# Sliding-window attention of a four-layer float32 kernel: keys and values from one feature-major product, values transposed, and a new order of projections and first scores

## The chip, the cores and the metric

The kernel runs on one core of a Trainium2 chip. The metric is the device time of one execution in microseconds (us), lower is better. The time before is 2381.49 us, the median of three runs (2381.35 to 2385.41).

## The reference, cut to what matters

The program computes a stack of transformer layers over 512 tokens of width 1024, all in float32. One of them is a mixer with causal sliding-window attention: 16 query heads of 64, two key/value heads (each shared by 8 query heads), a window of 128 tokens and one sink logit per head. Its input projection `w_in` has 1024 + 128 + 128 columns: queries, keys, values.

```python
def swa_sink_mixer(h, w_in, b_in, sinks, w_out, b_out):
    proj = h @ w_in + b_in
    q, k, v = jnp.split(proj, [1024, 1152], axis=-1)
    ...
    s = jnp.einsum('bnqkgd,bnskd->bnkgqs', q, kb) * (64 ** -0.5)
    s = jnp.where(valid[None, :, None, None], s, -jnp.inf)
    mx = jnp.maximum(jnp.max(s, axis=-1, keepdims=True), sink)
    e = jnp.exp(s - mx)
    p = e / (jnp.sum(e, axis=-1, keepdims=True) + jnp.exp(sink - mx))
    o = jnp.einsum('bnkgqs,bnskd->bnqkgd', p, vb)
    return o.reshape(B, T, 1024) @ w_out + b_out
```

Everything else in the program (a gated linear attention mixer, a state space mixer, a second attention mixer and four feed-forward parts) is left as it is.

## The kernel before, in words

**Precision.** Each float32 factor of a projection is split into a rounded part and its rest: AH and AL for activations, WH and WL for weights. A product is three matmuls, high by high, high by low, low by high (`three`, line 350).

**Weights.** The weights of the whole program are one stream of slabs of 128 rows and up to 512 columns. SyncE loads slab i into slot i mod 6 of WS (`weight_in`, line 286) once the rest of slab i - 6 is computed; ScalarE rounds it into WH (`weight_hi`, line 300) once slab i - 6 is no longer used; GpSimd computes the rest into WL (`weight_lo`, line 309). ScalarE and GpSimd do this six slabs ahead of TensorE: `weight_steps(put, e, w, name, nk, k0)` puts the slabs that lie six behind the slabs k0 to nk of part `name`. Each engine carries out its instructions in the order written, so where these steps stand among the other work of ScalarE and GpSimd matters.

**Products.** `gemm` (line 329) has two kinds. Kind "F" gives features by tokens: the weights are the stationary operand and 512 tokens move, in a PSUM bank per 128 features. Kind "T" gives tokens by features: 128 tokens are stationary, and the weights' columns move. `tail=n` runs the last n slabs bank by bank rather than slab by slab; `late=True` lets the first two banks start before the other two. `gemm` is a generator that yields after each slab, and the caller may put other work there. `held` names, per bank, what must be over before the bank is written again. BA is the banks 0 to 3, BB 4 to 7.

**The sliding attention.** `pe_swa`, `act_swa`, `dve_swa` and `pool_swa` (lines 1655 to 1761) are written by hand, one per engine. The order of TensorE is: queries 0 to 7 (`swa.q0`, kind F, 8 slabs of 512 columns, banks BB); keys (`swa.k`, kind F, 8 slabs of 256 columns, since each head's 64 columns are loaded twice, so that both halves of the partitions get a copy); queries 8 to 15 (`swa.q1`, kind F, banks BA); steps 0 and 1 of the attention; values (`swa.v`, kind T, 8 slabs of 128 columns, 96 matmuls), with attention step 2 behind slab 5; then steps 3 to 16. ScalarE and VectorE evict each query bank in two halves and two engines: `q_out` (ScalarE, line 1688) and `q_rest` (VectorE, line 1724).

**The attention pipeline.** `Attention` makes 14 pairs of banks of scores. For step u, TensorE (`pe_attention`, line 1469) computes scores u and adds the mask, transposes the first half of the probabilities of u - 2, multiplies the probabilities of u - 3 by the values, and transposes the second half of u - 2. VectorE (`dve_attention`, line 1571) reduces the maxima of u, copies a transposed half of u - 2 where u is odd, and divides the first half of u - 1. ScalarE (`act_attention`, line 1532) puts out a finished group, copies transposed halves of u - 2, and takes the exponentials of u. GpSimd divides the second half.

```python
run(gemm(... "swa.q1" ..., late=True))                   # line 1667
w.wait_ge(ve, "swa.q", 3)
pe_attention(e, w, SWA, held, range(2))
for kc in gemm(e, w, "swa.v", "T", ..., one_bank=True):
    if kc == 5:
        pe_attention(e, w, SWA, held, [2])
```

Of the kernel before, what the change touches and what calls it, by code (L numbers as in the profile page):

```python
# [9 lines left out]
F32 = mybir.dt.float32  # L10
# [21 lines left out]
V_MIXPRE, V_MLPPRE, V_BQ, V_BK, V_PSC, V_CW, V_CB, V_SN, V_QN, V_KN = 0, 16, 32, 40, 42, 46, 94, 106, 114, 118  # L32
NV = 120
R_BG, R_GN, R_BV, R_SINK, R_DTB, R_ALOG, R_DSK, R_FB = 0, 512, 768, 896, 912, 928, 944, 960
NR_ = 968
# [72 lines left out]
def program(nc, d, out):  # L108
    with ExitStack() as ctx:
# [219 lines left out]
        def gemm(e, w, name, kind, src, nk, xs, banks, ready, held, mw=P, head=None, tail=0, one_bank=False, late=False):  # L329

# [10 lines left out]
            def one(kc, m, weight, x, cs=slice(0, T), start=False, stop=False):  # L341
                s, n, b = (i0 + kc) % NS, width(i0 + kc), banks[m]
                if kind == "F":
                    return e.matmul(PS[b][0:mw, cs], weight[:, s, m * mw:(m + 1) * mw], x[:, cs], start=start, stop=stop,  # L344
                                    skip_group_check=head is not None)
                c = m * n if one_bank else 0
                return e.matmul(PS[b][:, c:c + n], x[:, m * P:(m + 1) * P], weight[:, s, 0:n], start=start, stop=stop,  # L347
                                skip_group_check=head is not None or one_bank)

            def three(kc, m):  # L350
                xh, xl = xs[kc]
                one(kc, m, WH, xh, start=kc == 0 and (m == 0 or not one_bank))
# [59 lines left out]
            for m in range(NT if tail else 0):  # L412
                for kc in range(k1, nk):
# [7 lines left out]
                    if kc == nk - 1:  # L421
                        q.then_inc(mm.sem, mm.tick("done", name, m))
                    elif m == NT - 1:
                        q.then_inc(mm.sem, mm.tick("used", i0 + kc))
# [1213 lines left out]
        def swa_group(t, kv):  # L1638
# [3 lines left out]
            def score(e, w, o, h, first):  # L1642
                w.wait_ge(ve, "swa.k", 1)
# [6 lines left out]
                        [sPT[:, j, :] for j in range(4)], [(mm, "done", "swa.v", 3)], True, 4, 0, 2, (ve, "swa.v"))  # L1650
# [4 lines left out]
        def pe_swa(e, w, held):  # L1655
# [5 lines left out]
            def ksrc(kc):  # L1661
                r = slice(kc * P, (kc + 1) * P)
                return [(64 * j, 64, sw[r, 1024 + 64 * (j // 2):1088 + 64 * (j // 2)]) for j in range(4)]
# [1124 lines left out]
```

## Time and profile before

| | before |
|---|---|
| median of 3 runs | 2381.49 us |
| the profiled execution's own time | 2381.4 us |
| span of its profile | 2379.6 us |
| TensorE busy | 2347.7 us (99%) |
| GpSimd, ScalarE, VectorE busy | 1079.5, 932.1, 701.2 us |
| mean granted TensorE clock | 0.999 |

The span runs from the first to the last instruction in the profile; the execution's own time is 1.8 us longer. A busy time is the union of an engine's instructions. The ends of matmuls are modelled and overlap the next start, so the distance of two starts tells what one costs, not its duration. "Idle before" gives the time in which an engine stood still ahead of a row and what ended it. The sliding attention with its projections lies between about 596 and 770 us.

### The profile page before, as it was taken

What the parts mean: (1) busy time and instruction counts of PE and PEld (TensorE: products, weight loads), DVE (VectorE), ACT (ScalarE), POOL (GpSimd) and SP (SyncE); (2) the same over time, 40 slices, a digit from 0 to 9 for tenths busy, and PEclk for the clock granted to TensorE, in tenths of its full rate; (3) what the DMA queues carried; (4) which work ended last, traced back from release to release, by engine and by line L of the source; (5) the groups of instructions that cost most, each with busy time, mean ns of one, the idle gap of its engine ahead of it and who ended that gap; (6) DMA issues with size and microseconds to landing.
All of it is one profiled execution on the core that took longest, in us unless ns stands there. A gap on an engine that the chain in (4) does not pass through costs nothing.

```text
span 2379.6 us, 29305 instructions
## 1 busy us (share of the span) xinstructions
PE 2347.7 (99%) x11545; PEld 1942.4 (82%) x11545; DVE 701.2 (29%) x1155; ACT 932.1 (39%) x1868; POOL 1079.5 (45%) x891
## 2 busy tenths in 40 slices
PE   9999999999999999999999999999999999999998
PEld 7888888888868888888887788888888778888887
DVE  3424320223284210314355331100152474100113
ACT  5524432334474432433445333323233572332331
POOL 5533544443434544454444444444444503544443
PEclk9999999999999999999999999999999999999999
DMA  6311323322312333333321333333233302433332
GB/s 187 86 62 54 117 96 98 98 98 62 89 36 87 113 98 98 93 102 94 93 85 41 98 111 98 98 93 102 88 98 89 80 1 81 132 98 98 95 97 74
DMA packets 161264, 215.08 MB, mean 90 GB/s; under 512 B 38063, under 2 KB 85927, under 8 KB 161127
## 3 DMA queue, kind: packets, MB, share of 16 engines
q1 hardware_dynamic: 157888, 204.10, 28.6%
q10 hardware_dynamic: 3239, 9.11, 1.2%
q8 instruction: 91, 1.49, 0.3%
q14 instruction: 46, 0.38, 0.0%
HBM read 210.53 MB, written 2.10 MB: 89 GB/s over the span
## 4 chain that ended last, share of the span: by engine, by line
PE 93%; DVE 3%; ACT 2%; POOL 1%; issue 1%; DMA 0%; SPq 0%; ACTq 0%; POOLq 0%; DVEq 0%
PE PS L344 44%; PE PS L347 40%; PE PS L1523 1%; PE PS L1501 1%; PE PS L464 1%; PE PS L2372 1%; ACT s_S L1564 0%; DVE X L586 0%; PE PS L2359 0%; DVE AL L499 0%; PE PS L2007 0%; PE PS L1064 0%; PE PS L445 0%; PE PS L1089 0%; PE PS L2363 0%
## 5 line engine op out<-in xcount | busy, mean ns | idle before, releaser
L318 POOL TENSOR_TENSOR WL<-WS,WH 128x512 fp32r<-128x512 f32 (+2 forms) x772 | 981.6, 1281 | 1089.6 <-ACT WH L307 1070.0
L307 ACT ACTIVATE WH<-WS 128x512 fp32r<-128x512 f32 (+2 forms) x774 | 476.6, 622 | 1217.4 <-PE PS L344 606.7
L344 PE MATMUL PS<-AH,WH 128*128 128x512 f32 (+1 forms) x1696 | 589.6, 373 | 2.9 <-ACT AH L481 2.3
L344 PE MATMUL PS<-AL,WH 128*128 128x512 f32 (+1 forms) x1696 | 586.5, 371 | 1.3 <-DVE AL L499 1.3
L344 PE MATMUL PS<-AH,WL 128*128 128x512 f32 x1552 | 581.7, 389 | 0.0
L344 PEld LDWEIGHTS PS<-AH,WH 128*128 128x128 f32 x1696 | 300.5, 188 | 59.5 <-ACT WH L307 2.8
L344 PEld LDWEIGHTS PS<-AL,WH 128*128 128x128 f32 x1696 | 300.6, 188 | 56.7 <-DVE AL L499 1.9
L344 PEld LDWEIGHTS PS<-AH,WL 128*128 128x128 f32 x1552 | 291.0, 188 | 60.6
L347 PE MATMUL PS<-WH,h_HL 128*128 128x512 f32 x864 | 336.1, 389 | 0.0
L347 PE MATMUL PS<-WH,h_HH 128*128 128x512 f32 x864 | 336.1, 389 | 0.0
L347 PE MATMUL PS<-WL,h_HH 128*128 128x512 f32 x864 | 336.1, 389 | 0.0
L347 PE MATMUL PS<-WH,AH 128*128 128x512 f32 (+2 forms) x616 | 229.4, 388 | 0.8 <-ACT g_G L1211 0.5
L347 PE MATMUL PS<-WH,AL 128*128 128x512 f32 (+2 forms) x616 | 224.4, 380 | 1.7 <-DVE AL L492 1.6
L347 PE MATMUL PS<-WL,AH 128*128 128x512 f32 (+2 forms) x616 | 222.1, 379 | 0.0
L347 PEld LDWEIGHTS PS<-WH,h_HL 128*128 128x128 f32 x864 | 162.2, 188 | 33.9
L347 PEld LDWEIGHTS PS<-WH,h_HH 128*128 128x128 f32 x864 | 162.2, 188 | 33.5
L347 PEld LDWEIGHTS PS<-WL,h_HH 128*128 128x128 f32 x864 | 162.2, 188 | 33.4
L826 DVE TENSOR_TENSOR h_HT<-h_HT 128x512 f32<-128x512 f32 x64 | 44.7, 699 | 418.9 <-ACT h_HH L803 418.9
L918 DVE TENSOR_TENSOR h_HT<-PS,h_HT 128x512 f32<-128x512 f32 x44 | 30.2, 687 | 395.0 <-ACT h_HT L893 395.0
L347 PEld LDWEIGHTS PS<-WH,AL 128*128 128x128 f32 x616 | 114.6, 188 | 24.5 <-DVE AL L492 2.6
L347 PEld LDWEIGHTS PS<-WH,AH 128*128 128x128 f32 x616 | 114.4, 188 | 23.6 <-issue 2.5
L347 PEld LDWEIGHTS PS<-WL,AH 128*128 128x128 f32 x616 | 114.7, 188 | 21.3 <-issue 0.7
(353 smaller groups left out, 1899.5 us busy)
## 6 DMA issues: line engine op xcount, KB each, us to landing
WS<-in_mlp_w_up_dram SPq DMA_DIRECT2D x128, 256.0 KB, 2.8
WS<-in_mlp_w_down_dram SPq DMA_DIRECT2D x128, 256.0 KB, 2.6
WS<-in_ffn_w_gate_dram SPq DMA_DIRECT2D x176, 128.0 KB, 2.1
WS<-in_ffn_w_up_dram SPq DMA_DIRECT2D x176, 128.0 KB, 2.2
WS<-in_ffn_w_down_dram SPq DMA_DIRECT2D x88, 256.0 KB, 2.6
WS<-in_gla_w_in_dram SPq DMA_DIRECT2D x48, 256.0 KB, 2.6
WS<-in_even_w_in_dram SPq DMA_DIRECT2D x48, 256.0 KB, 2.6
WS<-in_odd_w_in_dram SPq DMA_DIRECT2D x32, 256.0 KB, 2.7
```

The lines of the kernel that those rows point to most:

```text
L307: e.activation(WH[:, s, 0:n], WS[:, s, 0:n], ACT.Copy).then_inc(hi.sem, hi.tick(i))
L318: e.tensor_tensor(WL[:, s, 0:n], WS[:, s, 0:n], WH[:, s, 0:n].bitcast(F32), ALU.subtract).then_inc(lo.sem, lo.tick(i))
L344: return e.matmul(PS[b][0:mw, cs], weight[:, s, m * mw:(m + 1) * mw], x[:, cs], start=start, stop=stop, skip_group_check=head is not None)
L347: return e.matmul(PS[b][:, c:c + n], x[:, m * P:(m + 1) * P], weight[:, s, 0:n], start=start, stop=stop, skip_group_check=head is not None ...
L464: q = e.transpose(PS[b][:, (2 * c + t) * P:(2 * c + t + 1) * P], src(2 * half + t, 2 * j + c), IDENT)
L826: e.tensor_tensor(HT[:, k, :], HT[:, k, :], HT[:, k, :], ALU.mult).then_inc(ve.sem, ve.tick())
L918: e.tensor_tensor(HT[:, k, :], PS[b[2 + m]][:, :], HT[:, k, :], ALU.mult).then_inc(ve.sem, ve.tick("gated", name, n))
L1501: q = e.transpose(PS[b][:, j * P:(j + 1) * P], S[:, j * P:(j + 1) * P], IDENT)
L1523: q = e.matmul(o.rearrange("p (h n) -> p h n", h=per), G.v(2 * (c + i) + par, kb), p4[par][:, i:i + per, kb, :], start=kb == 0, stop=kb == ...
L2372: e.matmul(o, oMQ[:, h, t * P:W], oMK[:, h, 0:W], start=first, stop=False, skip_group_check=True)
```

## The change

- Keys and values come from one product of kind F (`swa.kv`, 8 slabs of 256 columns, banks 2 and 3, the last four slabs bank by bank). The keys' columns are loaded once, and ScalarE (`sKH`) and VectorE (`sKL`) write each head's keys to both halves of the partitions, in four half-width instructions each in the place of two whole ones.
- ScalarE evicts the values as features into `sVF` (a score buffer that is free then), TensorE transposes them in four instructions behind slab 1 of `swa.q1`, and VectorE copies them to `sV`. The bias is added on ScalarE. The product `swa.v` and its 8 slabs are gone.
- Attention steps 0 and 1 stand behind slabs 2 and 3 of `swa.q1`; its last four slabs then run bank by bank, and steps 2 to 16 follow without other work between.
- ScalarE: `q_out` of banks 0 to 2 behind attention step 1, of bank 3 behind step 2. VectorE: `q_rest` of banks 0 to 2 behind step 1, of bank 3 behind step 2. The weight steps placed at the attention's steps 8 and later are four in the place of six, on ScalarE and GpSimd.

```diff
         def pe_swa(e, w, held):
...
-            run(gemm(e, w, "swa.k", "F", ksrc, 8, AHL, BA[2:4], feats("mlp0"), held))
-            for m in range(2):
-                held[BA[2 + m]] = (ve, "swa.k", m)
-            run(gemm(e, w, "swa.q1", "F", cols(sw, 512, 512), 8, AHL, BA, feats("mlp0"), held, late=True))
+            run(gemm(e, w, "swa.kv", "F", cols(sw, 1024, 256), 8, AHL, BA[2:4], feats("mlp0"), held, tail=4))
+            held[BA[2]] = (ve, "swa.k", 1)
+            held[BA[3]] = (sc, "swa.vf")
+
+            def value_tokens():
+                b = BB[3]
+                w.wait_ge(*held[b])
+                w.wait_ge(sc, "swa.vf")
+                for t in range(NT):
+                    q = e.transpose(PS[b][:, t * P:(t + 1) * P], sVF[:, t * P:(t + 1) * P], IDENT)
+                q.then_inc(mm.sem, mm.tick("swa.v"))
+                held[b] = (ve, "swa.v")
+            for kc in gemm(e, w, "swa.q1", "F", cols(sw, 512, 512), 8, AHL, BA, feats("mlp0"), held, tail=4, late=True):
+                if kc == 1:
+                    value_tokens()
+                elif kc in (2, 3):
+                    pe_attention(e, w, SWA, held, [kc - 2])
             for m in range(4):
                 held[BA[m]] = (ve, "swa.q", 4 + m)
-            w.wait_ge(ve, "swa.q", 3)
-            pe_attention(e, w, SWA, held, range(2))
-            for kc in gemm(e, w, "swa.v", "T", cols(sw, 1152, 128), 8, AHL, [BA[3]] * 4, feats("mlp0"), held, one_bank=True):
-                if kc == 5:
-                    pe_attention(e, w, SWA, held, [2])
-            held[BA[3]] = (ve, "swa.v")
-            w.wait_ge(ve, "swa.q", 6)
-            pe_attention(e, w, SWA, held, range(3, SWA.n + 3))
+            pe_attention(e, w, SWA, held, range(2, SWA.n + 3))
...
         def act_swa(e, w):
...
-            run(weight_steps(weight_hi, e, w, "swa.k", 8))
-            for m in range(2):
-                w.wait_ge(mm, "done", "swa.k", m)
-                e.activation(sKH[:, m, :], PS[BA[2 + m]][:, :], ACT.Identity, bias=vcol(V_BK + m)).then_inc(
-                    sc.sem, sc.tick("swa.k", m))
-            run(weight_steps(weight_hi, e, w, "swa.q1", 8))
-            q_out(1, [3, 0])
-            act_attention(e, w, SWA, [0])
-            q_out(1, [1])
-            act_attention(e, w, SWA, [1])
-            late = weight_steps(weight_hi, e, w, "swa.v", 8)
-            next(late)
-            next(late)
-            q_out(1, [2])
+            run(weight_steps(weight_hi, e, w, "swa.kv", 4))
+            w.wait_ge(mm, "done", "swa.kv", 0)
+            for g in range(2):
+                r = slice(64 * g, 64 * g + 64)
+                for z in (g, 1 - g):
+                    e.activation(sKH[64 * z:64 * z + 64, g, :], PS[BA[2]][r, :], ACT.Identity,
+                                 bias=VC[r, V_BK:V_BK + 1]).then_inc(sc.sem, sc.tick("swa.k", g, z))
+            w.wait_ge(mm, "done", "swa.kv", 1)
+            e.activation(sVF, PS[BA[3]][:, :], ACT.Identity, bias=vcol(V_BV)).then_inc(sc.sem, sc.tick("swa.vf"))
+            run(weight_steps(weight_hi, e, w, "swa.kv", 8, 4))
+            for kc in weight_steps(weight_hi, e, w, "swa.q1", 4):
+                if kc > 1:
+                    act_attention(e, w, SWA, [kc - 2])
+            q_out(1, range(3))
+            late = weight_steps(weight_hi, e, w, "swa.q1", 8, 4)
             for u in range(2, SWA.n + 4):
                 act_attention(e, w, SWA, [u])
+                if u == 2:
+                    q_out(1, [3])
                 if u > 7:
                     next(late, None)
...
         def dve_swa(e, w):
...
-            q_rest(1, [3])
-            dve_attention(e, w, SWA, [0])
-            q_rest(1, [0])
-            dve_attention(e, w, SWA, [1])
-            q_rest(1, [1, 2])
-            dve_attention(e, w, SWA, [2])
-            w.wait_ge(mm, "done", "swa.v", 3)
...
+            w.wait_ge(mm, "swa.v")
+            e.tensor_copy(sV[:, :, :], PS[BB[3]][:, :].rearrange("p (t n) -> p t n", t=NT)).then_inc(
+                ve.sem, ve.tick("swa.v"))
+            dve_attention(e, w, SWA, [0, 1])
+            q_rest(1, range(3))
+            dve_attention(e, w, SWA, [2])
+            q_rest(1, [3])
             dve_attention(e, w, SWA, range(3, SWA.n + 4))
```

VectorE around attention steps 2 and 3, before. L1729 is `q_rest`, L1581 to L1593 the maxima of a step, L1607 to L1627 the division of the step before it, L1744 the values:

```order
L1729 SCALAR_TENSOR_TENSOR s_Q<-PS,VC,s_Q 64x512 x4
L1581 TENSOR_REDUCE SM<-PS 128x2 x2
L1589 SCALAR_TENSOR_TENSOR SM<-SM,NSINK 128x4
L1593 TENSOR_TENSOR SM<-ROWS,SM 128x4
L1607 TENSOR_TENSOR SM<-SM 128x4
L1611 RECIPROCAL SM<-SM 128x4
L1627 TENSOR_TENSOR s_S<-s_S,SM 128x512
L1744 TENSOR_TENSOR s_V<-PS,ROWS 128x512
L1581 TENSOR_REDUCE SM<-PS 128x2 x2
```

The same place with the change, where L1736 is `q_rest`, L1579 to L1591 the maxima and L1605 to L1625 the division:

```order
L1736 SCALAR_TENSOR_TENSOR s_Q<-PS,VC,s_Q 64x512 x6
L1579 TENSOR_REDUCE SM<-PS 128x2 x2
L1587 SCALAR_TENSOR_TENSOR SM<-SM,NSINK 128x4
L1591 TENSOR_TENSOR SM<-ROWS,SM 128x4
L1605 TENSOR_TENSOR SM<-SM 128x4
L1609 RECIPROCAL SM<-SM 128x4
L1625 TENSOR_TENSOR s_S<-s_S,SM 128x512
L1736 SCALAR_TENSOR_TENSOR s_Q<-PS,VC,s_Q 64x512 x2
L1579 TENSOR_REDUCE SM<-PS 128x2 x2
```

Between the division of step 2 and the maxima of step 3 two instructions of `q_rest` (bank 3) now stand where the eviction of the values stood.

ScalarE at the same steps, before. L1564 and L1569 are the exponentials of a step, L307 weights, L1694 `q_out`, L1552 copies of transposed probabilities:

```order
L1564 ACTIVATE s_S,SM<-PS,SM 128x256 x4
L1569 ACTIVATE SM<-SM 128x4
L307 ACTIVATE WH<-WS 128x128 x2
L1694 ACTIVATE s_Q<-PS,VC 64x512 x2
L1552 ACTIVATE s_PT<-PS 128x512 x2
L1564 ACTIVATE s_S,SM<-PS,SM 128x256 x4
L1569 ACTIVATE SM<-SM 128x4
L1552 ACTIVATE s_PT<-PS 128x512
```

With the change, where L1562 and L1567 are the exponentials, L1698 `q_out` and L1550 the copies:

```order
L1562 ACTIVATE s_S,SM<-PS,SM 128x256 x4
L1567 ACTIVATE SM<-SM 128x4
L1698 ACTIVATE s_Q<-PS,VC 64x512 x6
L1550 ACTIVATE s_PT<-PS 128x512 x2
L1562 ACTIVATE s_S,SM<-PS,SM 128x256 x4
L1567 ACTIVATE SM<-SM 128x4
L1698 ACTIVATE s_Q<-PS,VC 64x512 x2
L1550 ACTIVATE s_PT<-PS 128x512
```

`q_out` of bank 3 (L1698 x2) now stands behind the exponentials of step 2.

## Rows read from the trace of the kernel before

**Rows 1.** The page: busy time of the engines, and shares of the last chain by engine

```profile
PE 2347.7 (99%) x11545; PEld 1942.4 (82%) x11545; DVE 701.2 (29%) x1155; ACT 932.1 (39%) x1868; POOL 1079.5 (45%) x891
...
PE 93%; DVE 3%; ACT 2%; POOL 1%; issue 1%; DMA 0%; SPq 0%; ACTq 0%; POOLq 0%; DVEq 0%
```

**Rows 2.** Chain in order of time (start us, us, what): 512-column matmuls, then the values

```profile
410.77 87.04 PE PS L344 x384
...
649.36 7.99 PE PS L347 x72
...
658.81 0.93 PE PS L1501 x8
659.74 2.63 PE PS L347 x24
```

**Rows 3.** Timeline of TensorE (start us, us, what), attention steps 0 to 6, first instructions

```profile
645.54 0.22 PE L1645 MATMUL PS<-s_KH,s_Q 128*128 128x128 f32 x1
...
647.71 0.36 PE L1645 MATMUL PS<-s_KH,s_Q 128*128 128x256 f32 x1
...
649.12 0.31 PE L347 MATMUL PS<-WH,AH 128*128 128x128 f32 x1
...
657.19 0.33 PE L1645 MATMUL PS<-s_KH,s_Q 128*128 128x256 f32 x1
...
658.64 1.09 PE L1501 MATMUL PS<-CK,s_S 128*128 128x128 f32 x8
...
662.20 0.33 PE L1645 MATMUL PS<-s_KH,s_Q 128*128 128x256 f32 x1
...
667.73 0.63 PE L1501 MATMUL PS<-CK,s_S 128*128 128x128 f32 x4 [0.48 <-ACT AH L1540]
...
675.28 0.63 PE L1501 MATMUL PS<-CK,s_S 128*128 128x128 f32 x4 [0.47 <-DVE s_S L1627]
```

**Rows 4.** Timeline of VectorE, attention steps 2 and 3

```profile
658.52 1.53 DVE L1729 SCALAR_TENSOR_TENSOR s_Q<-PS,VC,s_Q 64x512 fp32r<-64x512 f32 x2 [1.96 <-ACT s_Q L1694]
660.08 1.29 DVE L1581 TENSOR_REDUCE SM<-PS 128x2 f32<-128x512 f32 x2
...
662.08 0.69 DVE L1627 TENSOR_TENSOR s_S<-s_S,SM 128x512 f32<-128x512 f32 x1
...
663.63 1.29 DVE L1581 TENSOR_REDUCE SM<-PS 128x2 f32<-128x512 f32 x2 [0.26 <-PE PS L1489]
...
665.88 0.69 DVE L1601 COPY s_PT<-PS 128x512 f32<-128x512 f32 x1 [0.57 <-PE PS L1501]
...
666.89 0.69 DVE L1627 TENSOR_TENSOR s_S<-s_S,SM 128x512 f32<-128x512 f32 x1
```

**Rows 5.** Timeline of ScalarE, attention steps 2 and 3

```profile
657.09 1.39 ACT L1694 ACTIVATE s_Q<-PS,VC 64x512 fp32r<-64x512 f32 x2
659.28 1.09 ACT L1552 ACTIVATE s_PT<-PS 128x512 f32<-128x512 f32 x2 [0.80 <-PE PS L1501]
...
665.15 0.48 ACT L1564 ACTIVATE s_S<-PS,SM 128x256 f32<-128x256 f32 x1 [0.27 <-DVE SM L1589]
...
667.06 0.60 ACT L1540 ACTIVATE AH<-PS 128x512 fp32r<-128x512 f32 x1
```

**Rows 6.** Timeline of ScalarE, weight slabs rounded while the keys' product runs

```profile
619.14 2.82 ACT L307 ACTIVATE WH<-WS 128x256 fp32r<-128x256 f32 x6
```

**Rows 7.** Timeline of GpSimd, rests of the same slabs

```profile
619.63 8.94 POOL L318 TENSOR_TENSOR WL<-WS,WH 128x256 fp32r<-128x256 f32 x8 [5.24 <-ACT WH L307]
```

**Rows 8.** Chain in order of time, ScalarE at attention step 12

```profile
701.82 1.82 ACT s_S L1564 x8
703.74 0.52 ACT WH L307
```

**Rows 9.** Timeline of TensorE, the row behind its longest idle

```profile
706.71 0.63 PE L1501 MATMUL PS<-CK,s_S 128*128 128x128 f32 x4 [1.94 <-ACT s_S L1564]
```

**Rows 10.** Windows: us, busy PE, PEld, DVE, ACT, POOL, PEclk, DMA share, GB/s

```profile
700.00:710.00 10.00, 7.39 (x58) 4.93 (x54) 9.08 (x19) 8.33 (x27) 6.16 (x6) 1.00 0.18 56
```

More of the change, by code:

```diff
@@ L325, in weight_steps, with gemm @@
                 yield kc
-        def gemm(e, w, name, kind, src, nk, xs, banks, ready, held, mw=P, head=None, tail=0, one_bank=False, late=False):
+        def gemm(e, w, name, kind, src, nk, xs, banks, ready, held, mw=P, head=None, tail=0, late=False):
             if name not in first:
@@ L345, in one @@
                                     skip_group_check=head is not None)
-                c = m * n if one_bank else 0
-                return e.matmul(PS[b][:, c:c + n], x[:, m * P:(m + 1) * P], weight[:, s, 0:n], start=start, stop=stop,
-                                skip_group_check=head is not None or one_bank)
+                return e.matmul(PS[b][:, 0:n], x[:, m * P:(m + 1) * P], weight[:, s, 0:n], start=start, stop=stop,
+                                skip_group_check=head is not None)
             def three(kc, m):
                 xh, xl = xs[kc]
-                one(kc, m, WH, xh, start=kc == 0 and (m == 0 or not one_bank))
+                one(kc, m, WH, xh, start=kc == 0)
                 if kind == "F":
@@ L411, in gemm @@
                 yield kc
-            for m in range(NT if tail else 0):
+            for m in range(count(k1) if tail else 0):
                 for kc in range(k1, nk):
@@ L422, in gemm @@
                         q.then_inc(mm.sem, mm.tick("done", name, m))
-                    elif m == NT - 1:
+                    elif m == count(kc) - 1:
                         q.then_inc(mm.sem, mm.tick("used", i0 + kc))
@@ L1642, in score @@
             def score(e, w, o, h, first):
-                w.wait_ge(ve, "swa.k", 1)
+                w.wait_ge(ve, "swa.k", kv)
+                w.wait_ge(ve, "swa.q", 4 * kv + 3)
                 q, ks = sQ[:, 8 * kv + h, t * P:(t + 1) * P], slice(k0 * P, k0 * P + W)
@@ L1649, in program @@
         SWA = Attention("swa", [swa_group(t, kv) for kv in range(2) for t in range(NT)], [sS[:, j, :] for j in range(6)],
-                        [sPT[:, j, :] for j in range(4)], [(mm, "done", "swa.v", 3)], True, 4, 0, 2, (ve, "swa.v"))
+                        [sPT[:, j, :] for j in range(4)], [(mm, "done", "swa.q1", 3)], True, 4, 0, 2, (ve, "swa.v"))
+        sVF = sS[:, 5, :]
         def hn(name):
@@ L1751, in pool_swa @@
         def pool_swa(e, w):
-            for part in ("swa.q0", "swa.k", "swa.q1"):
-                run(weight_steps(weight_lo, e, w, part, 8))
-            late = weight_steps(weight_lo, e, w, "swa.v", 8)
-            next(late)
-            next(late)
+            for part, nk in (("swa.q0", 8), ("swa.kv", 8), ("swa.q1", 4)):
+                run(weight_steps(weight_lo, e, w, part, nk))
+            late = weight_steps(weight_lo, e, w, "swa.q1", 8, 4)
             for x in range(SWA.n):
```

28 lines of the change are left out of this document (12 added, 16 removed).

## The prediction, written before the changed kernel was run

> **What bounds the kernel now.** I read the page first. TensorE is busy 2347.7 of 2379.6 us and holds 93% of the chain that ended last, so a change gains where it takes work from TensorE and no wait comes in its place [rows 1]. Next the chain in order of time over the stage: matmuls of 512 columns follow each other 87.04 / 384 = 0.227 us apart, and the product of the values is on the chain too, as pieces of 7.99 and 2.63 us [rows 2]. Last the timelines of the engines around attention steps 2 and 3, since the steps are a pipeline through four engines and the change moves its fill: the starts of each step on TensorE [rows 3], and what VectorE and ScalarE do for it [rows 4, 5]. The reader is to see there that the attention runs at about 3.8 us a step (two steps from 667.73 to 675.28, with only 0.47 us idle at the second [rows 3]): TensorE bounds it, but barely, so work on TensorE that is lost can't be made up later, and a hole stays a hole.
>
> **The change, part by part.** I count us from the start of a step's scores. All of it is set against the profiled execution: 2381.4 us, 1.8 us over its span, which is also the median (2381.49) within 0.1 us.
>
> *The values' product goes.* 96 matmuls take 7.99 + 2.63 = 10.6 us on the chain [rows 2]. They move only 128 columns each and still start 10.62 / 96 = 0.111 us apart. Keys and values now take 8 slabs of two banks, 48 matmuls of 512 columns, exactly what the keys took alone: nothing is added there. The Trainium skill ("TensorE: Matmul & The Clock Gate", section "Wait — 56ns, not 53.3ns?") has warm back-to-back matmuls of 128 columns start 55.6 ns apart. By that figure, as an estimate, the product would be worth 96 x 0.0556 = 5.3 us and the whole gain 5.3 us smaller; the trace's distance is twice that and the measurement is what I use.
>
> *Four transposes come in.* Eight take 0.93 us [rows 2], so four with a changeover take about 0.6 us. They wait for the eviction of the values as features, priced below.
>
> *Steps 0 and 1 move into `swa.q1`.* Their work stays: 2.17 us (645.54 to 647.71) and 1.41 us (to 649.12) [rows 3]. Their exponentials and divisions now lie beside the last four slabs, 48 matmuls of 512 columns: 48 x 0.227 = 10.9 us (12 for each bank, 2.72 us). That covers the softmax of both. Step 2 begins when these end: 645.54 + 0.6 + 2.17 + 1.41 = 649.7, against 657.19 before, 7.5 us earlier.
>
> *Step 2 and 3 lose their filler.* Before, 2.7 us of the values' product stood between steps 2 and 3, and bank 3 was still free of queries. Now, from 649.7 as zero:
> - TensorE: scores 0 to 1.45 (657.19 to 658.64), transposes of step 0 to 2.3 (x8, 0.9), scores of 3 from 2.3 [rows 3].
> - VectorE: maxima of 2 start 1.43 behind the scores' start (662.20 to 663.63 [rows 3, 4]); the division of step 1 starts 2.00 behind them (660.08 to 662.08 [rows 4]), at 3.43; the transpose that waits for it follows 0.84 later (666.89 to 667.73 [rows 3, 4]), at 4.27. TensorE was ready at 3.75: idle 0.5 us.
> - ScalarE: two copies end at about 3.05 (658.64 + 0.64, then 1.09 with overlap [rows 3, 5]); the exponentials of step 2 last 1.91 (665.15 to 667.06 [rows 5]), to 4.98. Only now comes `q_out` of bank 3, though its bank was complete at 0.
> - VectorE waits for both halves: `q_rest` starts 1.43 behind `q_out` (657.09 to 658.52 [rows 4, 5]), at 6.4, and takes 1.56, to 7.97. Only now come the maxima of step 3, whose scores have lain there since 3.7. From there to the division of step 2 it is 3.26 (663.63 to 666.89) less the 0.57 that its copy waited [rows 4]: 10.65. The transposes of step 2 start at 11.5, that is at 661.2.
> - TensorE meanwhile does the transposes of step 1 and the product of step 0, and the scores of step 4, and is done at about 7.7. It is idle 3.75 us.
>
> Before, the same transposes started at 667.73 [rows 3]. So this point comes 6.5 us earlier. The check by work: 10.6 out, 0.6 in, new idles 0.5 + 3.75, old idle 0.48 gone, gives 6.3. I take **6.5**. Who waits for the queued work: nobody needs bank 3's queries before step 8; the cost is the order of the queues alone.
>
> *Behind that point* VectorE, ScalarE and TensorE stand to each other as before: maxima of step 4 start 0.2 us ahead of these transposes then and now. The lead of 6.5 us stays.
>
> *The end of the attention.* ScalarE's weight step at attention step 12 is on the chain with 0.52 us, between exponentials [rows 8]. Two of six such steps (the ones at 12 and 13) are gone. I take **0.5**; the bounds are 0 (another wait steps in) and 1.0 (both count).
>
> *Keys, evictions, weights: nothing.* ScalarE has four half evictions of keys (0.70 each by the pair of 1.39 [rows 5]) where two whole ones stood, and one of the values, 3.5 us in all, ahead of the slabs 2 to 5 of `swa.q1`. Its slabs end at about 622 [rows 6]; the keys' bank is complete 2.72 before the product ends at 623.8 (645.54 less 96 matmuls of 0.227), so it evicts from 621.3 to 624.8 and rounds slab 2 by 625.4. GpSimd takes 8.94 / 8 = 1.1 to 1.3 us a slab [rows 7]: ready at 626.8. TensorE asks for it 24 matmuls and four transposes behind 623.8, at 629.8. The cover is 3 us; if it were gone, each us late would be a us lost. The rests of the keys on VectorE end at about 625.9; the bank is written again at 626.5. SyncE issues fewer loads and waits for nothing new.
>
> **Sum.** 6.5 + 0.5 = 7.0 us: span 2372.6, time 2374.4.
>
> **The rivals.**
> 1. *The hole doesn't open.* If the steps overlap better than my chain, for example because step 3's division isn't what TensorE stands before, the gain is 10.6 - 0.6 + 0.5 = 10.5: 2370.9. For it speaks that TensorE's share is 99%; against, that VectorE's order is fixed and its wait for bank 3 is written in. 12%.
> 2. *The hole is deeper.* Step 3's exponentials end as late as the hole, and step 5 needs their banks; a second wait of 1 to 3 us would leave a gain of 4 to 6: 2375.4 to 2377.4. Against: step 5's scores start some 2 us behind the hole, the exponentials are over by then. 12%.
> 3. *The weights come late.* If ScalarE's evictions ate the cover of 3 us and 3 more, 2377. 5%.
> 4. *Slower: TensorE's clock falls in the hole.* TensorE's longest idle now is 1.94 us [rows 9] and the granted clock in those 10 us is 1.00, the upper level, 2.4 GHz [rows 10]; a hole of 3.75 us is new to this kernel. At the lower level, 1.2 GHz, TensorE's work of a step, 3.8 less at most 0.5 idle, 3.3 us, would double: each step at that level costs 3.3 us. One leaves 2377.7, two 2381.0; from the third the change is slower, 2384.3, and at four 2387.6. The skill's page named above, section "Why this matters for your kernels", says that a long idle between bursts of matmuls sends the engine back to the lower level; no run here shows a hole of this length. By that rule, which speaks against this change, one or two steps would be slow. 8%, half of it with three steps or more.
>
> **How the numbers follow.** Forecast 63%, rivals 12, 12, 5 and 8%. The time is the forecast's, 2374.4. The range holds the forecast, rival 1 and most of rival 2 and 3: 2370.8 to 2378.5; outside lie most of rival 4 and some mishap, under 15%. A measurement of this kernel can tell about 0.2% (4.8 us) from no change. Faster than 2376.7 are the forecast, rival 1 and half of rival 2: 0.79. Within 4.8 us of before are the rest of rivals 2, 3 and part of 4: 0.17. Slower by more: four slow steps, 0.04.
>
> **What would show it right or wrong.** No 128-column matmuls of line 347's kind in the stage; step 2's scores 7.5 us earlier; an idle of 3 to 4 us on TensorE before the transposes of step 2, with VectorE waiting for ScalarE's `q_out` and then the maxima of step 3 about 4 us after their scores; the first matmul of the output product 7 us earlier. Wrong would be: an idle behind slab 1 of `swa.q1` (weights), a granted clock under 1.00, or no such hole.

## The result, and the profile after

| | before | after |
|---|---|---|
| median, same session, 20 runs each | 2385.36 us (2381.3 to 2386.38) | 2377.98 us (2376.63 to 2382.84) |
| mean of these runs | 2384.05 us | 2379.47 us |
| the profiled execution's own time | 2381.4 us | 2377.84 us |
| span of its profile | 2379.6 us | 2376.0 us |
| mean granted TensorE clock in the profile | 0.999 | 0.998 |

The ratio is 0.9981, with a 95% interval of 0.9975 to 0.9987: 0.19% faster, just inside the 0.2% that a measurement can tell from no change. It is the ratio of the means, which differ by 4.6 us; the medians differ by 7.4. The profiled executions differ by 3.6 us, where 7.0 were forecast. The page's rows that answer to [rows 1]:

```profile
PE 2340.4 (99%) x11453; PEld 1933.5 (81%) x11453; DVE 701.7 (30%) x1157; ACT 932.3 (39%) x1863; POOL 1076.5 (45%) x883
...
PE 92%; DVE 4%; ACT 2%; issue 1%; POOL 1%; DMA 0%; SPq 0%; ACTq 0%; POOLq 0%; DVEq 0%
```

TensorE has 92 matmuls fewer (96 out, 4 in) and is busy 7.3 us less, and of the span only 3.6 us are gone. The timeline of TensorE after the change, for the rows of [rows 3] and [rows 9]; the bracket is the idle time before the row and what ended it:

```profile
620.33 0.50 PE L343 MATMUL PS<-AH,WH 128*128 128x512 f32 x1 [0.55 <-POOL WL L318]
...
650.59 0.28 PE L1644 MATMUL PS<-s_KH,s_Q 128*128 128x256 f32 x1
...
662.06 1.09 PE L1499 MATMUL PS<-CK,s_S 128*128 128x128 f32 x4 [3.62 <-DVE s_S L1625]
...
672.26 0.63 PE L1499 MATMUL PS<-CK,s_S 128*128 128x128 f32 x4 [0.48 <-ACT AH L1538]
...
703.71 0.63 PE L1499 MATMUL PS<-CK,s_S 128*128 128x128 f32 x4 [1.95 <-ACT s_S L1562]
...
709.17 1.08 PE L1521 MATMUL PS<-s_PT,s_V 128*64 128x256 f32 x8 [0.88 <-DVE s_PT L1599]
```

The lead over before shrinks along these rows. The scores of step 2 start at 650.59 against 657.19, 6.60 earlier. The transposes of step 2 come at 662.06 against 667.73, 5.67 earlier, behind the forecast hole: 3.62 us. The transposes of step 4 come at 672.26 against 675.28, only 3.02 earlier: between two points where TensorE had nearly the same work as before, 2.65 us were lost. Windows of the same stretch tell why (us, busy PE, PEld, DVE, ACT, POOL, PEclk, DMA share, GB/s):

```profile
655.00:660.00 5.00, 3.44 (x24) 2.12 (x22) 2.84 (x5) 2.60 (x8) 0.79 (x1) 1.00 0.00 0
660.00:668.00 8.00, 5.94 (x27) 4.33 (x28) 4.88 (x14) 4.96 (x19) 2.08 (x2) 0.57 0.01 2
668.00:680.00 12.00, 11.52 (x100) 8.89 (x97) 9.09 (x24) 9.44 (x39) 2.08 (x2) 1.00 0.00 1
```

Inside the hole, at 661.0 us, the granted clock fell from 1.00 to 0.50 (2.4 to 1.2 GHz) and stayed there for 6.83 us. Four transposes that took 0.63 us before take 1.09 [rows 3]. In the profile of before the clock does not fall until the very end of the span, at 2374.7 us. The busy time above contains this slow stretch: the kernel below whose hole is half filled, and whose clock stayed up, is busy 2339.9 us with 1.6 us of thrown-away work in it, so without that it has 9.4 us less work than before, by this estimate, where the prediction had 10.0 (10.6 out, 0.6 in). The hole itself, in the timeline of VectorE after the change, answering to [rows 4]:

```profile
651.98 1.29 DVE L1579 TENSOR_REDUCE SM<-PS 128x2 f32<-128x512 f32 x2 [0.94 <-PE PS L1487]
...
657.07 1.53 DVE L1736 SCALAR_TENSOR_TENSOR s_Q<-PS,VC,s_Q 64x512 fp32r<-64x512 f32 x2 [2.40 <-ACT s_Q L1698]
658.63 1.29 DVE L1579 TENSOR_REDUCE SM<-PS 128x2 f32<-128x512 f32 x2
...
661.23 0.69 DVE L1625 TENSOR_TENSOR s_S<-s_S,SM 128x512 f32<-128x512 f32 x1
```

and of ScalarE, answering to [rows 5]:

```profile
652.63 1.08 ACT L1550 ACTIVATE s_PT<-PS 128x512 f32<-128x512 f32 x2 [3.16 <-PE PS L1499]
...
653.74 0.47 ACT L1562 ACTIVATE s_S<-PS,SM 128x256 f32<-128x256 f32 x1
...
655.64 1.39 ACT L1698 ACTIVATE s_Q<-PS,VC 64x512 fp32r<-64x512 f32 x2
```

Bank 3's queries were complete when the scores of step 2 began, at 650.59, but ScalarE evicts them only at 655.64, behind the exponentials of step 2. VectorE stands still for 2.40 us, and the maxima of step 3 and the division of step 2 (661.23) follow late. That is the forecast chain.

### The profile page after: what moved, and what is told of

Read it like the earlier page. It is cut to its first block, busy times and chain, and to the rows that moved or that the text cites. A ratio compares the mean times of both kernels' runs of the same rounds, so it can differ in the third digit from the quotient of the medians.

```text
span 2376.0 us, 29065 instructions
## 1 busy us (share of the span) xinstructions
PE 2340.4 (99%) x11453; PEld 1933.5 (81%) x11453; DVE 701.7 (30%) x1157; ACT 932.3 (39%) x1863; POOL 1076.5 (45%) x883
## 4 chain that ended last, share of the span: by engine, by line
PE 92%; DVE 4%; ACT 2%; issue 1%; POOL 1%; DMA 0%; SPq 0%; ACTq 0%; POOLq 0%; DVEq 0%
PE PS L343 44%; PE PS L345 40%; PE PS L1521 1%; PE PS L1499 1%; PE PS L462 1%; PE PS L2377 1%; DVE SM L1579 0%; DVE X L584 0%; PE PS L2364 0%; DVE AL L497 0%; ACT s_S L1562 0%; POOL Y L2331 0%; PE PS L1062 0%; PE PS L443 0%; PE PS L1087 0%
## 5 line engine op out<-in xcount | busy, mean ns | idle before, releaser
L307 ACT ACTIVATE WH<-WS 128x512 fp32r<-128x512 f32 (+1 forms) x766 | 474.0, 625 | 1203.6 <-PE PS L345 602.2
L345 PE MATMUL PS<-WH,AH 128*128 128x512 f32 (+1 forms) x584 | 220.6, 394 | 0.8 <-ACT g_G L1209 0.5
L345 PE MATMUL PS<-WH,AL 128*128 128x512 f32 (+1 forms) x584 | 215.6, 386 | 1.7 <-DVE AL L490 1.6
L345 PE MATMUL PS<-WL,AH 128*128 128x512 f32 (+1 forms) x584 | 213.3, 384 | 0.0
L345 PEld LDWEIGHTS PS<-WH,AL 128*128 128x128 f32 x584 | 108.4, 188 | 24.5 <-DVE AL L490 2.6
L345 PEld LDWEIGHTS PS<-WH,AH 128*128 128x128 f32 x584 | 108.3, 188 | 23.4 <-issue 2.5
L345 PEld LDWEIGHTS PS<-WL,AH 128*128 128x128 f32 x584 | 108.6, 188 | 21.4 <-issue 0.7
```

What stands on the lines that cost most here:

```text
L307: e.activation(WH[:, s, 0:n], WS[:, s, 0:n], ACT.Copy).then_inc(hi.sem, hi.tick(i))
L345: return e.matmul(PS[b][:, 0:n], x[:, m * P:(m + 1) * P], weight[:, s, 0:n], start=start, stop=stop, skip_group_check=head is not None)
```

## The experiments

Each kernel's whole time mixes this stage with the clock in later stages, so I read two numbers for each: the time against before, and the stage's lead, which is the start of the attention's last product (709.17 above; before, L1523 at 712.71) against before's.

```profile
712.71 1.08 PE L1523 MATMUL PS<-s_PT,s_V 128*64 128x256 f32 x8 [0.88 <-DVE s_PT L1601]
```

By that measure the change leads by 3.54 us.

### Is it the clock? Keep TensorE busy through the hole

Rival theories: the clock fell in the hole (2.65 us), or the pipeline behind the hole lost its rhythm by itself. Fourteen matmuls of 512 columns whose results are thrown away are put ahead of the wait that makes the hole.

```diff
+                        if name == "swa" and v == 2 and par == 0:
+                            for _ in range(14):
+                                e.matmul(PS[b][:, :], sKH[:, 0, 0:P], sQ[:, 0, :], start=True, stop=True,
+                                         skip_group_check=True)
                         w.wait_ge(A.divider(par), "prob", name, v, par)
```

> The change, with 14 idle-time matmuls of 512 columns (results thrown away, overwritten by the transposes) put on TensorE before the transposes of attention step 2, where it stood idle for 3.62 us; nothing else is touched. Clock theory: the hole is filled with 14 x 0.227 = 3.2 us, the granted clock stays 1.00 through the stage, the transposes of step 2 still start near 662.1, and all that follows comes 2.65 us earlier than in the change: span about 2373.3, the transposes of step 4 near 669.6 instead of 672.26. Rival (the later steps are late because VectorE and ScalarE were thrown out of step by the hole, not because of the clock): the transposes of step 4 stay near 672.3 and the span near 2376.

Measured: 2380.41 us, median of 11 (2375.16 to 2380.74), ratio 0.9975 (0.9967 to 0.9984). The timeline of TensorE and the windows of this kernel:

```profile
661.94 0.66 PE L1503 MATMUL PS<-CK,s_S 128*128 128x128 f32 x4 [0.34 <-DVE s_S L1629]
...
669.52 0.63 PE L1503 MATMUL PS<-CK,s_S 128*128 128x128 f32 x4 [0.48 <-DVE s_S L1629]
...
700.96 0.88 PE L1503 MATMUL PS<-CK,s_S 128*128 128x128 f32 x4 [1.95 <-DVE s_S L1629]
```

```profile
660.00:668.00 8.00, 7.66 (x57) 5.57 (x56) 6.78 (x19) 6.88 (x27) 2.08 (x2) 1.00 0.00 0
700.00:705.00 5.00, 4.04 (x20) 2.57 (x20) 2.79 (x6) 1.86 (x8) 2.08 (x2) 0.66 0.14 51
1290.00:1310.00 20.00, 18.75 (x87) 15.28 (x87) 14.58 (x22) 11.01 (x34) 10.34 (x9) 0.83 0.00 0
1740.00:1750.00 10.00, 8.10 (x49) 7.59 (x48) 8.51 (x11) 3.48 (x7) 5.10 (x7) 0.83 0.42 112
```

With no useful work added and no wait shortened, the granted clock stays at 1.00 and the transposes of step 4 come at 669.52 in the place of 672.26. Of these 2.74 us, 0.12 were there at step 2 already (661.94 against 662.06); the other 2.62 are the clock's. The stage's lead is only 4.7, because in this run the clock fell at 701.2 (from step 12 to the last product it took 7.04 us where the change took 5.46), and it fell again near 1300 and 1746, in code that none of these kernels touches. By the mean clocks that is also why its median is above the change's 2377.98: 6 of its 11 runs stand at 2380.4 to 2380.8 us with a mean clock of 0.996, while 12 of the change's 20 runs stand at 2376.6 to 2378.1. Lowest against lowest, it is 2375.16 against 2376.63; the high levels are 2380.5 against 2382.1 to 2382.8.

**Half the filler.** The same with 7 in the place of 14. It asks whether a shorter idle at this place leaves the clock up.

```diff
-                            for _ in range(14):
+                            for _ in range(7):
```

> The change with 7 thrown-away matmuls of 512 columns (1.6 us) in the hole before the transposes of step 2, half of what filled it, so that about 2.0 us of idle are left, as long as the idle of 1.95 us that the kernel always had at step 12. If the fall of the clock hangs on the length of the idle stretch: no fall at 661, the transposes of step 4 near 669.6 and the lowest runs at 2375.2 as with the hole filled. Rival (any hole of that kind does it): the clock is at 0.5 behind 662 and the transposes of step 4 start near 672.

Measured: 2381.14 us, median of 11 (2375.68 to 2383.52), ratio 0.9981 (0.9972 to 0.999). Timeline and window:

```profile
662.51 0.66 PE L1503 MATMUL PS<-CK,s_S 128*128 128x128 f32 x4 [1.91 <-DVE s_S L1629]
...
670.09 0.63 PE L1503 MATMUL PS<-CK,s_S 128*128 128x128 f32 x4 [0.47 <-DVE s_S L1629]
```

```profile
660.00:668.00 8.00, 6.09 (x48) 4.18 (x46) 6.99 (x19) 6.31 (x23) 2.08 (x2) 1.00 0.00 0
```

In this profile an idle of 1.91 us costs no clock, where one of 3.62 us does. (Everything from 9 us on stands 0.6 later in it, long before the edit; less that, step 4 is at 669.5, as with the full filler.) It is one execution, the quickest: 3 of the 11 runs stand at 2383.3 to 2383.5 us, 1.5 us or more over all others, with a mean clock of 0.995 that none of the 11 runs with the full filler has. Where their clock fell is not on record, so it is not shown that half the filler always suffices.

**The same hole with a shorter fall.** Two kernels further below (the weight steps moved, and `tail=3`) keep the hole at 3.63 us. Their clock fell there too, but for 3.41 us instead of 6.83. Transposes of steps 2 and 4 and the window, for the first of them:

```profile
662.12 0.63 PE L1499 MATMUL PS<-CK,s_S 128*128 128x128 f32 x4 [3.63 <-ACT s_S L1562]
...
671.21 0.63 PE L1499 MATMUL PS<-CK,s_S 128*128 128x128 f32 x4 [0.48 <-ACT AH L1538]
```

```profile
660.00:668.00 8.00, 5.88 (x36) 4.60 (x38) 5.83 (x16) 5.86 (x22) 2.08 (x2) 0.79 0.00 0
```

From step 2 to step 4 it takes 9.09 us there (9.13 with `tail=3`), where the change takes 10.20 and before, like both fillers, 7.55 to 7.58. So behind one and the same hole 3.41 us at the lower level cost 1.5 us and 6.83 us cost 2.65: the loss goes with the clock and not with the hole. All three profiles with this hole have the fall, and none of the six in which it is filled or shorter has one there.


### Is it the order of the evictions? Bank 3 ahead of step 2

```diff
-            q_out(1, range(3))
+            q_out(1)
...
                 act_attention(e, w, SWA, [u])
-                if u == 2:
-                    q_out(1, [3])
```

> The change, with ScalarE's eviction of query bank 3 ahead of its attention step 2 in the place of behind it (ScalarE stood idle for 3.16 us there). VectorE's part stays where it is. Queue theory: VectorE no longer waits 2.40 us for it, the maxima of step 3 come 2.5 us earlier (about 656.1 for 658.63), the hole on TensorE shrinks from 3.62 to 1.1 us, the clock stays at 1.00, and the gain over the change is 2.5 + 2.65 = 5.1 us: span about 2371. If the clock falls at short holes too: gain 2.5 us, span 2373.5. Rival (the hole comes from the softmax of step 2 and not from bank 3): the hole stays above 3 us, span 2376.

Measured: 2376.94 us, median of 5 (2374.44 to 2377.06), ratio 0.9966 (0.9953 to 0.9978).

```profile
659.70 0.63 PE L1499 MATMUL PS<-CK,s_S 128*128 128x128 f32 x4 [1.26 <-DVE s_S L1625]
...
667.25 0.63 PE L1499 MATMUL PS<-CK,s_S 128*128 128x128 f32 x4 [0.48 <-DVE s_S L1625]
```

```profile
660.00:668.00 8.00, 7.52 (x61) 5.57 (x61) 6.76 (x18) 6.38 (x24) 2.53 (x3) 1.00 0.00 1
```

The hole is 1.26 in the place of 3.62, the clock stays, and the stage's lead is 8.56 us (the last product starts at 704.15): 5.0 more than the change. 2.36 of them are the hole, 2.65 its clock. One eviction in its queue had cost 5.0 of these 8.6 us. The whole time shows less of it: 4 of the 5 runs stand at 2376.9 to 2377.1, since the clock fell near 1295 and 1773 us (table below). Set against before by the ratios, 0.9966 and 0.9981, some 3.6 us are left.

### The weights: one slab later into the keys' tail

The 0.55 us idle at 620.33 is TensorE waiting for the rest of a weight slab in `swa.kv`. Run bank by bank, the last four slabs are asked for sooner than ScalarE and GpSimd bring them.

```diff
-            run(gemm(... "swa.kv", ..., held, tail=4))
+            run(gemm(... "swa.kv", ..., held, tail=3))
```

> The change, with tail=3 for tail=4 in the product of keys and values, so that TensorE asks for slab 6 0.68 us later. Theory: the idle of 0.55 us at 620.33 (waiting for GpSimd's rest of slab 6) goes, everything behind comes 0.5 us earlier, span 2375.5, the clock falls as in the change. Rival (the evictions of the keys bound the start of the third bank of the next product, so the time is only moved): the idle comes back near 626, span 2376.

Measured: 2381.69 us, median of 11 (2377.12 to 2382.58), ratio 0.9983 (0.9975 to 0.9992). Timeline of TensorE:

```profile
620.49 0.50 PE L343 MATMUL PS<-AH,WH 128*128 128x512 f32 x1
...
661.64 0.92 PE L1499 MATMUL PS<-CK,s_S 128*128 128x128 f32 x4 [3.63 <-DVE s_S L1625]
```

No idle at 620 any more, and the stage runs 0.4 us ahead of the change as far as the hole (661.64 against 662.06). The hole is as in the change, but the fall behind it lasted 3.41 us and not 6.83, and the whole run shows nothing of the 0.4, since the clock fell at 703, 1300 and 1778 too.

### The values' product alone, without the new order

Values as features and transposed, but queries 8 to 15 whole, then steps 0, 1, 2 and on, with ScalarE's and VectorE's evictions as before and all weight steps ahead of the attention (the edits of these engines are left out here).

```diff
-            for kc in gemm(... "swa.q1", ..., tail=4, late=True):
+            for kc in gemm(... "swa.q1", ..., late=True):
...
-                elif kc in (2, 3):
-                    pe_attention(e, w, SWA, held, [kc - 2])
...
-            pe_attention(e, w, SWA, held, range(2, SWA.n + 3))
+            pe_attention(e, w, SWA, held, range(SWA.n + 3))
```

> One part of the change alone: keys and values in one product and the values transposed, but the queries' product run whole before attention step 0 and the evictions in the order of before. Theory (the new order is what makes the shorter product worth something): with no work behind steps 0 and 1, TensorE stands idle for about 4 us before the scores of step 2, until the exponentials of step 0 free their banks; the clock falls there too. Of 10.6 us taken out, 0.6 + 0.5 come back as transposes and late weights, 4 to 5 as idle and about 3 by the clock: span 2377.5 to 2379.5. Rival (the order is worth nothing, the work taken out decides): span near the change's, 2376, or below.

Measured: 2386.49 us, median of 11 (2381.91 to 2387.85), ratio 1.0001 (0.9992 to 1.001). No gain at all; I had expected part of it. Timeline and window:

```profile
655.38 0.55 PE L1644 MATMUL PS<-s_KH,s_Q 128*128 128x256 f32 x1 [4.52 <-ACT SM L1567]
...
664.35 0.63 PE L1499 MATMUL PS<-CK,s_S 128*128 128x128 f32 x4 [2.19 <-DVE s_S L1625]
```

```profile
655.00:661.00 6.00, 5.62 (x26) 5.37 (x27) 4.20 (x10) 5.90 (x18) 1.04 (x1) 0.50 0.00 0
```

The 10.6 us of the values' product had covered the softmax of the first steps. Taken out alone, it leaves idles of 4.52 and 2.19 us and a clock at half for 6.83 us at 654.7 and 3.41 us at 665.0, and the stage ends 2.4 us later than before. By an estimate from these rows, 10.0 us less work, 0.55 lost at 620 and 6.7 of idle would leave 2.7 us at the full clock; no profile of this order kept the clock, so that is not shown. As it ran, the smaller product was worth nothing without the new order.

### The end of the attention: weight steps

ScalarE's and GpSimd's four weight steps moved from the attention's steps 8 to 11 to steps 10 to 13, where before had some.

```diff
-                if u > 7:
+                if u > 9:
...
-                if x > 7:
+                if x > 9:
```

> The change with its last four weight steps of ScalarE and GpSimd at attention steps 10 to 13 for 8 to 11, that is, back at the end where the kernel before had them. Theory (the gain at the end of the attention, 0.54 us between the transposes of step 12 and the last product, comes from there being no weight step at 12 and 13): that distance is again 6.0 us for 5.46. Rival (it comes from elsewhere): it stays 5.46.

One run, 2377.08 us:

```profile
702.44 0.63 PE L1499 MATMUL PS<-CK,s_S 128*128 128x128 f32 x4 [1.94 <-ACT s_S L1562]
...
708.45 1.08 PE L1521 MATMUL PS<-s_PT,s_V 128*64 128x256 f32 x8 [0.88 <-DVE s_PT L1599]
```

From the transposes to the last product it takes 6.01 us, before 6.00 (706.71 to 712.71), the change 5.46: the weight steps that are gone at 12 and 13 are worth 0.54 us. Its lead at the end, 4.26, is larger than the change's, since its clock fell for 3.41 us at 663.4 and not for 6.83.

### Three mends together, and step 2 inside the projection

Bank 3 early, `tail=3`, and the weight steps at 5 to 8:

```diff
-                if u > 7:
+                if u > 4:
```

> The change with three repairs: query bank 3 evicted by ScalarE ahead of its step 2, tail=3 in the product of keys and values, and the last four weight steps of ScalarE and GpSimd at attention steps 5 to 8 for 8 to 11. If the parts add: the stage ends 8.57 us before the kernel before (as with bank 3 alone) plus 0.5 (late weights) plus 0.3 to 0.5 (weight steps off the end of the attention), 9.4 us in all. Where the clock stays up everywhere that is a span of 2370.2 and a time of 2372.0; where it falls in the later stages, some 2 to 4 us more, as in the kernel before. Rival: the earlier weight steps meet the query evictions on ScalarE and reopen a hole, then the stage gives 8 us or less.

Measured: 2376.5 us, median of 6 (2376.29 to 2377.9), ratio 0.9966 (0.9953 to 0.9978). Timeline and window:

```profile
659.20 0.63 PE L1499 MATMUL PS<-CK,s_S 128*128 128x128 f32 x4 [1.26 <-DVE s_S L1625]
...
698.17 0.63 PE L1499 MATMUL PS<-CK,s_S 128*128 128x128 f32 x4 [1.88 <-DVE s_S L1625]
...
704.88 1.08 PE L1521 MATMUL PS<-s_PT,s_V 128*64 128x256 f32 x8 [0.87 <-DVE s_PT L1599]
```

```profile
698.00:703.00 5.00, 4.83 (x26) 3.15 (x28) 2.03 (x5) 2.43 (x7) 2.08 (x2) 0.66 0.00 0
```

The first point is 8.5 us ahead of before (659.20 against 667.73), but the clock falls at 699.1, behind the 1.88 us idle, and the lead ends at 7.8, where 9.4 were expected.

Then step 2's scores ahead of the last bank of the product, and `q_rest` of banks 2 and 3 behind VectorE's steps 2 and 3, on top of two of the three: `tail=3` and the weight steps. ScalarE's `q_out` of bank 3 stays behind its step 2. (`second` runs inside `gemm`, ahead of the last bank; that edit is left out here.)

```diff
+            def second():
+                for m in range(3):
+                    held[BA[m]] = (ve, "swa.q", 4 + m)
+                pe_attention(e, w, SWA, held, [2])
...
-            q_rest(1, range(3))
+            q_rest(1, range(2))
             dve_attention(e, w, SWA, [2])
+            q_rest(1, [2])
+            dve_attention(e, w, SWA, [3])
```

> The change with attention step 2 inside the last four slabs of swa.q1, ahead of bank 3 (so 2.72 us of matmuls lie between steps 2 and 3), VectorE's q_rest of banks 2 and 3 behind its steps 2 and 3, and the weight repairs of the kernel with three repairs. Theory (what is missing behind step 2 is work on TensorE): no idle over 1 us up to step 5, the clock stays up, the stage ends 10 us before the kernel before: 0.5 to 1 us better than the three repairs. Rival (VectorE's evictions are only moved, and their 3 us come out at step 4): an idle of 1.5 us or more at step 4, no better than the three repairs.

Measured: 2377.37 us, median of 5 (2375.94 to 2377.5), ratio 0.9967 (0.9954 to 0.9979). Timeline:

```profile
657.82 0.63 PE L1501 MATMUL PS<-CK,s_S 128*128 128x128 f32 x4 [0.48 <-ACT AH L1540]
659.29 1.08 PE L1523 MATMUL PS<-s_PT,s_V 128*64 128x256 f32 x8 [0.84 <-DVE s_Q L1742]
```

The 1.26 us idle became 0.48 + 0.84, the second because VectorE's `q_rest` now stands ahead of its copy. The lead at the last product is 8.0, where 10 were expected, and 0.2 more than with the three mends: not worth its complexity.

### The best of them, with the clock held at step 12

The three mends, with 7 thrown-away matmuls ahead of the wait at step 12 (the longest idle left).

```diff
+                        if name == "swa" and v == 12 and par == 0:
+                            for _ in range(7):
+                                e.matmul(PS[b][:, :], sKH[:, 0, 0:P], sQ[:, 0, :], start=True, stop=True,
+                                         skip_group_check=True)
```

> The kernel with three repairs, with 7 thrown-away matmuls of 512 columns (1.6 us) in the idle of 1.88 us before the transposes of step 12. Clock theory: the fall near 700 that cost the three repairs 1.2 us of the stage is gone, the stage ends 9.1 us before the kernel before; the falls near 1296 and 1774 stay. Lowest runs near 2372.3 where nothing falls, median 1.2 us under that of the three repairs (2376.5). Rival (the matmuls run on into the transposes, or the fall near 700 has another cause): no gain, stage at 7.8 us.

Measured: 2374.27 us, median of 5 (2372.82 to 2377.01), ratio 0.9955 (0.9942 to 0.9967): some 11 us under before, faster than both kernels.

```profile
698.72 0.60 PE L1503 MATMUL PS<-CK,s_S 128*128 128x128 f32 x4
...
704.15 1.08 PE L1525 MATMUL PS<-s_PT,s_V 128*64 128x256 f32 x8 [0.88 <-DVE s_PT L1603]
```

```profile
694.00:704.00 10.00, 8.98 (x63) 5.74 (x61) 6.18 (x15) 7.03 (x25) 3.12 (x3) 1.00 0.00 0
```

From step 12 to the last product: 5.43 us, against 6.71 in the kernel without the filler (698.17 to 704.88). That fall cost 1.3 us. That the filler prevented it is not shown: these are two single profiles, and with bank 3 early alone the clock stayed up at this place behind an idle of 1.95 us and no filler. The falls near 1296 and 1774, expected to stay, are missing in this profile too, with no edit there, and it is the quickest of the five runs; two others stand at 2377. The intervals of this kernel and of the three mends without filler overlap.

### Before once more: is its stage constant?

Since the times of before ranged over 5 us, I took a second profile of it, unchanged.

> The kernel before, unchanged, looked at again, for where its own runs differ (2381.4, 2385.5 and 2386.3 us). Clock theory: in a run of 2385 or more the granted clock is at 0.5 for some us near 1300 and 1750 us (and perhaps near 705), where the first profile had 1.00 throughout, and every us of difference to the first profile arises there. Rival: the difference is spread over the span.

2382.39 us, with one fall of the clock, for 3.41 us at 706.6:

```profile
706.70 1.09 PE L1501 MATMUL PS<-CK,s_S 128*128 128x128 f32 x4 [1.95 <-ACT s_S L1564]
```

```profile
700.00:710.00 10.00, 8.05 (x52) 5.03 (x49) 9.07 (x18) 7.41 (x25) 6.17 (x6) 0.83 0.17 54
```

The row and the window answer to [rows 9] and [rows 10], where the same idle left the clock at 1.00. It starts at 706.70 against 706.71, and the last product at 713.70 against 712.71: the whole difference of the two profiles, 1.0 us, is this fall. The run was none of those at 2385 us or more, so the falls that I expected near 1300 and 1750 in such a run of before are not shown by a profile.

### How the falls spread one kernel's times

The lead over before's profile at three points of the program, matched by the same VectorE instruction, counted from the last one (at 754, 1322 and 2374 us of before):

| kernel | 754 us | 1322 us | 2374 us | falls of the clock between, at (for) us |
|---|---|---|---|---|
| after | 3.55 | 3.57 | 3.59 | none |
| bank 3 early | 8.57 | 6.14 | 4.52 | 1295 (6.83), 1773 (3.41) |
| 14 thrown away | 4.72 | 2.31 | 0.65 | 1299 (6.83), 1746 (3.41) |
| three mends | 7.84 | 5.41 | 3.76 | 1296 (6.83), 1774 (3.41) |
| three mends, filled | 8.59 | 8.61 | 8.57 | none |

In the stretches where no fall stands the lead is kept to 0.04 us over 1600 us. A fall near 1300 costs 2.4 us, one near 1750 or 1773 costs 1.6. The levels of before's own runs fit that: 2381.4 to 2381.6 us at a mean granted clock of 0.999, 2382.4 to 2384.0 at 0.998, 2385.4 to 2385.7 at 0.997, 2385.9 to 2386.6 at 0.996; in the session of the two kernels with 7 thrown away they lie higher, from 2381.92 at 0.999 to 2387.46 at 0.996. Compared at equal clocks, 0.999: before 2381.4, the kernel with 14 thrown away 2375.16 (6.2 less), the one with 7 in the hole 2375.68 (6.2 less than its own session's 2381.92), the last one 2372.82 (9.1 less than the same 2381.92). The last row of the table is lower than these 9.1, since everything in that profile stands 0.6 later from 9 us on.

## Why the prediction was right and wrong

**The values' product and the transposes: right.** At the full clock TensorE's work fell by 9.4 us, where 10.0 were forecast, and the two values' pieces are gone from the chain. At equal clock the kernel with 14 thrown away is 6.2 us under before.

The figure of the Trainium skill that I had set aside ("TensorE: Matmul & The Clock Gate", section "Wait — 56ns, not 53.3ns?", 55.6 ns for 128 columns) would have left a sum of 7.0 - 5.3 = 1.7 us, as an estimate; the 6.2 us measured speak for the trace's 0.111 us.

**"7.5 us earlier" for step 2: 0.9 too much.** It was 6.60 (650.59). The step that failed is "Keys, evictions, weights: nothing". I worked out the cover of the slabs of `swa.q1` (3 us, and none came late) and not that of the slabs inside the tail of `swa.kv`, where running bank by bank asks for a slab sooner. That cost 0.55 us; removing the tail's fourth slab gave 0.4 back. The values' transposes are not the rest: they took 0.36 us (630.06 to 630.42), less than the 0.6 forecast. The remaining 0.35 us stay unexplained; no run splits them.

**The hole: right.** From step 2's scores to its transposes I forecast 11.5 us, and it took 11.47; idle 3.75 forecast, 3.62 measured, with the cause named. The small idle before, 0.5, was 0.38. Moving one eviction confirmed the cause. I had computed the hole and put its cost at its length alone.

**"The lead of 6.5 us stays": this step failed.** The sum had the clock behind the hole at nothing. The lead fell from 5.67 to 3.02, because the clock was at 0.50 for 6.83 us. This was rival 4, to which I gave 8%. Its mechanism came as described, one step at the lower level, and its price of 3.3 us was 0.65 too high against 2.65 measured. That its time of 2377.7 and the measured 2377.84 agree is luck, since a lead that was already 0.8 smaller than forecast makes up for the price. The chance was what was wrong. I reasoned from an idle of 1.94 us at a clock of 1.00 [rows 9, 10] that a hole of 3.75 might pass too, though it was twice as long as any idle in the trace. The profile shows the fall, and of the 20 runs of the change none has a mean clock of 0.999, while of before's 27 runs beside the first experiments 5 have. The rule of the Trainium skill that I quoted ("TensorE: Matmul & The Clock Gate", section "Why this matters for your kernels") spoke against the change, and the trace agrees with it: 0.50 behind 3.62 us idle. Other falls of this record came without a long idle, so the rule alone would not have found them.

**The end of the attention, 0.5: right**, 0.54 measured and taken back by moving the weight steps. Rival 1 (no hole) and rival 2 (a second wait behind it) did not come: the next idle is 0.48 us, at 672.26. Rival 3 came in a small form, 0.55 us, and in another product than the one I named.

**The sum.** Forecast 7.0: minus 0.83 for the late start, minus 2.65 for the clock, minus 0.02 from step 4 to step 12, plus 0.04 at the end, gives 3.54, the measured lead of the stage. It is then carried unchanged to the end (3.6 in the span). With the clock kept up the change is worth 6.2 us. That the median lies in the range (2370.8 to 2378.5) is partly luck: 12 of the change's 20 runs are inside, 8 stand at 2382.1 to 2382.8, beyond it. That the medians differ by 7.4 us, nearly the 7.0 forecast, is luck as well: 12 of before's 20 runs stand 4 to 5 us over its quickest, so its median is one of its high levels and the change's one of its low ones. Against the 2381.49 us that stood ahead of the prediction the gain is 3.5. The ratio, 0.9981, is case "same", to which I gave 0.17. Two small slips in the prediction change nothing here: rival 3 comes to 2377.4 and not 2377, and the chances of a faster kernel add to 0.81 and not 0.79.

**What stays open.** Why the clock falls near 700, 1300 and 1750 us in some runs and not in others, while at 661 it fell in all three profiles with the long hole and by the mean clocks seems to fall in every run of the change. Near 700, 1300 and 1746 there are idles of 1.95, 1.2 and 1.6 us ahead, in the profiles without a fall too. Near 1773 there is none: with bank 3 early TensorE is busy throughout the 27 us ahead, at its end with 20 matmuls of 8 columns (a window, and a row of the timeline in it):

```profile
1746.00:1773.00 27.00, 27.00 (x151) 23.45 (x150) 8.44 (x15) 11.41 (x20) 19.95 (x19) 1.00 0.55 160
...
1770.62 2.29 PE L2415 MATMUL PS<-o_F,CK 128*128 128x8 f32 x20
```

No edit here separates that. That the falls in the kernel with the values' part alone come from its two idles is argued from the rows; I did not fill those to show it.

## What to carry to other kernels

On an engine that is 99% busy, price a new hole twice: its idle, and the clock behind it, if it is longer than any idle the trace shows at full clock. The change's hole of 3.6 us cost 2.65 us more by the clock. Look for the hole's cause in a queue: here an eviction whose bank had long been complete stood behind a step's exponentials, and moving it brought the stage 5.0 us forward, more than the 3.5 of the whole change. Work that leaves TensorE may have been the cover of a start-up, so take it out together with a new order; and judge changes of a few us by the start of a marked instruction in the stage and by runs of equal mean clock, not by medians alone.

## What the runs showed of the hardware that I had not expected

- The granted clock fell to 0.50 (1.2 GHz) for 6.83 or 3.41 us at a time. Behind an idle of 3.62 or 3.63 us at 661 it fell in three profiles of three, behind 1.91 us at the same place it did not in the one profile taken, behind 1.95 us at 706 it did in one profile of before and not in the other (1.94 us). Near 1773 it fell with no idle in the 27 us ahead.
- The measured cost was at most half of the time at the lower level: 6.83 us cost 2.65 at 661 and 2.4 near 1300, 3.41 us cost 1.5 at 661 to 663, 1.0 to 1.6 near 700 and 1.6 near 1750. That other engines bound the rest of the time is argued, not shown.
- Matmuls whose results are thrown away, in the place of the hole, went with a clock that stayed up: 14 of them brought the following work 2.6 us forward.
- One unchanged kernel has times at several levels from 2381.4 to 2386.6 us (to 2387.5 in another session), and each goes with a mean granted clock from 0.999 to 0.996.
